# Mixed values made behind the last differential probabilities, output accumulators taken at first use, modulation sums over quadrants in one product per group

## Chip, cores and metric

The kernel runs on one core of one Trainium2 chip. The metric is device microseconds (us) for one execution. The kernel before takes 1186.48 us, the median of three runs (1186.45, 1186.48 and 1188.06). TensorE is called PE below, VectorE DVE, ScalarE ACT, GpSimd POOL, and SyncE SP, whose queue issues most of the loads.

## What is computed

256 tokens of width 1024 go through two blocks, all in float32. The first block has two encoder layers. Each does

```
h    = rmsnorm(x, norm_g[l])
proj = h @ w_in[l]                    # q, k, v, gate of two attentions, 4096 columns
out_a = neighborhood_attention(...)   # 8 heads of 64, a window of 16 columns of a 4 x 64 grid
out_b = diff_attention(...)           # 4 heads: softmax 1 - lam * softmax 2, times v, then rmsnorm
y = concat(out_a * silu(g_a), out_b * silu(g_b))
x = x + y @ w_out[l]
```

The second block has two layers of three sublayers: a SwiGLU feed forward (1024 to 2 x 2816 and back), a mixer (a pooling one in layer 0, attention on shared keys and values in layer 1), and another feed forward. Each sublayer normalizes x and modulates it with a shift, a scale and a gate, which are parts of `silu(c) @ ada_w[layer] + ada_b[layer]`. With the two vectors of the shared keys and values that makes 20 modulation vectors of 1024 values each.

## The kernel before

**Products.** A float32 product is made of three fp32r products: the high part of the activations times the high part of the weights (L1893), low times high (L1898), high times low (L1906). ACT makes the high part of each weight unit (w_hi, L666, a unit is 128 x 2048), and DVE (L1222) or POOL (L535, in four pieces) makes the low part (w_lo = raw - w_hi). `half_step` (L1879) issues one such step of 12 matmuls for one unit and one half of the tokens. A step takes about 2.7 us. Each engine's order is written out by hand; semaphores, named by events, link the engines.

**Encoder layer.** `column_product` (L1938) runs 32 steps s = 0 to 31, four for each of 8 column groups (`IN_GROUPS`, L82): q and k of the differential attention (kind b), v b, q a, k a, v a, gate b, gate a. Group g accumulates in one of two pairs of PSUM banks; `acc_use` (L1857) makes the PE queue wait until the group that used the pair two uses ago is freed. The group v a (g = 5) ends with s = 23. Behind every step each engine does the short work of the attentions that the table `short_work` (L417) puts there, in the same order on all engines. Around the change that is:

- s = 23: `da_pT` of head 3 (the differential probabilities of the last head are transposed by PE, L2073, and copied from PSUM by ACT, L738), then `na_scores` of pair 1.
- s = 24: `da_out` of head 3 (PE, L2106: probabilities times v b; it waits for the copy of s = 23), then `na_pT` of pair 0 (PE L2082, ACT copy L738).
- s = 25: `na_out` of pair 0 (PE, L2094). It waits for event `v_ready` of kind a and for the copy of s = 24. Then `na_scores` of pair 2.

**Mixed values.** The neighborhood attention of a row block reads 128 keys that lie in both token tiles, so beside v a itself (`vv["a"]`, shown as va) two mixed tiles `v_mix` are made from the same PSUM banks. They lie in the memory of the differential queries, so the profile shows them as qbT. ACT makes them in its work at the end of group 5, ahead of everything else of s = 23: two copies of 128 rows (L878), the copy to va (L868 in layer 0, in two halves, L866 in layer 1, in one), then two copies of 32 rows (L878) behind a wait on the first two. Only then comes the copy of the probabilities (L738).

**Output product.** Behind s = 31 the loop behind L2148 takes two pairs of banks, for both token tiles, at its start: the first is freed by `gate_ready` b, the second by `gate_ready` a, which DVE (L1526) signals after ACT's tanh of the last group. It runs eight steps. Between step 0 and step 1, and between 1 and 2, PE transposes the gated neighborhood output (L1990), for which it waits for `y_gated` a (DVE L1416 in layer 0, L1413 in layer 1).

**Modulation sums.** DVE multiplies and adds the rows of `ada_w` by silu(c) (`ada`, L1195), transposes the 128 partial sums of a vector in blocks of 32 x 32 (L1154) and reduces each block (L1157) into `parts`: for partition p and block b a sum over a quarter of the rows. What is left is a sum over the four quadrants of 32 partitions. `FOLDS` (L53) groups the 20 vectors into eight folds of 1 to 4 vectors. For each fold, `fold_sums` (L1915) issues four float32 matmuls with four shifted 128 x 128 views of `fold` (zeros, and a column block that adds up the quadrants) and with every fourth column of `parts`, and DVE's `reduce_vectors` (L1162) adds the bias in one instruction (L1167) and finishes each vector. `fold` is zeroed by POOL and filled by one DVE instruction (`fold_columns`, L1144). The first fold lies behind s = 31 of layer 0, the other seven in the feed forward products.

`job` (L1847) gives the PSUM banks 4, 5 and 6 in turn to the short work; each use waits until the one before on that bank is read.

## Time and profile before

| | us |
|---|---|
| median of three runs | 1186.48 |
| lowest and highest | 1186.45, 1188.06 |
| the profiled execution, device time | 1186.72 |
| its span in the trace | 1184.9 |
| PE busy with matmuls | 1161.9 (98%) |
| DVE busy | 823.6 (70%) |
| ACT busy | 583.4 (49%) |
| POOL busy | 564.6 (48%) |

The profiled execution lies 0.24 us above the median, and 1.8 us of it lie outside the span. A row of a timeline gives the start, the length, the engine, the line, and the instruction with its tiles and their shapes; x4 means that four instructions were merged, and the brackets name the idle time ahead of it and what ended it. PE's rows overlap, since the length of a matmul contains its way through the array: the distance of two starts is the time that it takes up.

### The profile page before, as it was taken

The page shows a single profiled execution, that of the slowest core. Times are in us where ns is not written, and L with a number is a line of the kernel's source. Part 1 is how long each engine was busy: PE and PEld are TensorE (multiplying, and loading weights), DVE is VectorE, ACT ScalarE, POOL GpSimd, SP SyncE. Part 2 cuts the span into 40 slices and gives each one's busy share as a digit, 9 for nine tenths or more (in the row PEclk, how much of TensorE's full clock was granted, in tenths as well). Part 3 has the DMA queues.
Part 4 walks back from the last instruction along what each step waited for, and adds up shares of the span by engine and source line. Part 5 has one row for each costly group of instructions (what it writes and reads, how often), then busy time and mean ns, then how long its engine had stood idle before and what let it go on. Part 6 is the DMA issues. An engine that isn't in the chain of part 4 may idle for free.

```text
span 1184.9 us, 15260 instructions
## 1 busy us (share of the span) xinstructions
PE 1161.9 (98%) x5688; PEld 952.7 (80%) x5688; DVE 823.6 (70%) x1152; ACT 583.4 (49%) x764; POOL 564.6 (48%) x418
## 2 busy tenths in 40 slices
PE   9999999999999999899999999999999999999998
PEld 6777787877788888888887888888888887888887
DVE  6896468856797797778769666797793666645423
ACT  5557564676543443644344267443342766443440
POOL 1365324575364552735535227665351563445360
PEclk9999999999999999999999999999999999999999
DMA  9976379846799997569898658799874534876650
GB/s 349 352 273 223 111 250 333 279 150 221 235 368 323 330 348 292 163 214 344 276 333 313 239 209 285 249 345 301 311 288 143 186 123 160 267 232 203 204 195 36
DMA packets 183833, 297.93 MB, mean 251 GB/s; under 512 B 8464, under 2 KB 102352, under 8 KB 183760
## 3 DMA queue, kind: packets, MB, share of 16 engines
q1 hardware_dynamic: 177696, 284.82, 69.7%
q10 hardware_dynamic: 6064, 12.14, 3.1%
q8 instruction: 46, 0.75, 0.3%
q14 instruction: 27, 0.22, 0.1%
HBM read 294.79 MB, written 2.13 MB: 251 GB/s over the span
## 4 chain that ended last, share of the span: by engine, by line
PE 84%; DVE 8%; ACT 4%; issue 2%; SPq 1%; DMA 1%; POOL 1%; ACTq 0%; DVEq 0%
PE ps L1893 26%; PE ps L1906 25%; PE ps L1898 25%; PE ps L2188 2%; PE ps L1990 1%; DVE w_lo L1222 1%; ACT w_hi L666 1%; DVE ps L1206 1%; DMA raw<-w_in 1%; PE ps L2047 1%; POOL stat L526 1%; PE ps L2106 1%; SPq L492 1%; PE ps L2036 1%; DVE ps L1318 1%
## 5 line engine op out<-in xcount | busy, mean ns | idle before, releaser
L535 POOL TENSOR_TENSOR w_lo<-raw,w_hi 128x512 fp32r<-128x512 f32 x348 | 485.4, 1427 | 428.3 <-ACT w_hi L666 428.1
L666 ACT ACTIVATE w_hi<-raw 128x2048 fp32r<-128x2048 f32 x188 | 354.5, 1909 | 102.3 <-PE ps L1906 68.2
L1893 PE MATMUL ps<-w_hi,h_hi 128*128 128x512 f32 x1120 | 313.0, 401 | 1.0 <-issue 0.8
L1906 PE MATMUL ps<-w_lo,h_hi 128*128 128x512 f32 x1120 | 301.4, 391 | 0.8 <-DVE w_lo L1222 0.4
L1898 PE MATMUL ps<-w_hi,h_lo 128*128 128x512 f32 x1120 | 300.5, 390 | 0.0
L1222 DVE TENSOR_TENSOR w_lo<-raw,w_hi 128x2048 fp32r<-128x2048 f32 x96 | 225.2, 2350 | 103.6 <-ACT w_hi L666 101.3
L1906 PEld LDWEIGHTS ps<-w_lo,h_hi 128*128 128x128 f32 x1120 | 209.3, 188 | 48.4 <-DVE w_lo L1222 2.7
L1898 PEld LDWEIGHTS ps<-w_hi,h_lo 128*128 128x128 f32 x1120 | 210.3, 188 | 45.9 <-DVE h_lo L1282 0.2
L1893 PEld LDWEIGHTS ps<-w_hi,h_hi 128*128 128x128 f32 x1120 | 202.3, 189 | 43.5 <-issue 5.5
L1206 DVE SCALAR_TENSOR_TENSOR ps<-ada_raw,ccol,ps 128x512 f32<-128x512 f32 x240 | 181.1, 754 | 7.9 <-DMA ada_raw<-ada_w 1.1
L950 ACT ACTIVATE a_hi<-ps 128x512 fp32r<-128x512 f32 x44 | 26.4, 599 | 156.4 <-PE ps L2188 156.4
L526 POOL TENSOR_TENSOR stat<-stat,minus_half 128x1 f32<-128x1 f32 (+3 forms) x25 | 29.1, 1166 | 147.9 <-DVE stat L1258 112.3
L1893 PE MATMUL ps<-w_hi,a_hi 128*128 128x512 f32 x348 | 94.0, 392 | 0.0
L1906 PE MATMUL ps<-w_lo,a_hi 128*128 128x512 f32 x348 | 93.1, 389 | 0.0
L1898 PE MATMUL ps<-w_hi,a_lo 128*128 128x512 f32 x348 | 93.1, 389 | 0.0
L1898 PEld LDWEIGHTS ps<-w_hi,a_lo 128*128 128x128 f32 x348 | 65.3, 188 | 13.7
L1906 PEld LDWEIGHTS ps<-w_lo,a_hi 128*128 128x128 f32 x348 | 65.3, 188 | 13.7
L1893 PEld LDWEIGHTS ps<-w_hi,a_hi 128*128 128x128 f32 x348 | 64.6, 188 | 12.9
L960 ACT ACTIVATE hn<-ps 128x512 f32<-128x512 f32 x44 | 26.3, 598 | 92.9 <-PE ps L1906 92.9
L1580 DVE SCALAR_TENSOR_TENSOR hn<-hn,ps 128x512 f32<-128x512 f32 x44 | 30.1, 685 | 45.0 <-ACT hn L960 44.8
L760 ACT ACTIVATE pr<-lg,stat 128x256 f32<-128x256 f32 (+1 forms) x64 | 28.5, 447 | 52.2 <-DVE stat L1366 52.2
L1573 DVE TENSOR_TENSOR a_lo<-ps,a_hi 128x512 fp32r<-128x512 f32 x44 | 30.4, 692 | 32.3 <-ACT a_hi L950 31.2
(209 smaller groups left out, 964.1 us busy)
## 6 DMA issues: line engine op xcount, KB each, us to landing
raw<-ffn_in SPq DMA_DIRECT2D x176, 512.0 KB, 5.9
ada_raw<-ada_w SPq DMA_DIRECT2D x144, 512.0 KB, 7.3
raw<-ffn_out SPq DMA_DIRECT2D x44, 1024.0 KB, 6.6
raw<-w_in SPq DMA_DIRECT2D x31, 1024.0 KB, 8.4
raw<-w_out SPq DMA_DIRECT2D x8, 1024.0 KB, 5.0
ada_raw<-kv_ada_w SPq DMA_DIRECT2D x16, 512.0 KB, 7.9
raw<-w_kv SPq DMA_DIRECT2D x8, 1024.0 KB, 5.7
raw<-w_q SPq DMA_DIRECT2D x4, 1024.0 KB, 5.1
```

The source lines that it names most:

```text
L526: pool.tensor_tensor(st(at, n), st(at, n), minus_half[:, 0:n], ALU.pow).then_inc(*S.inc("rsqrt_ready", *key))
L535: ins = pool.tensor_tensor(w_lo[:, u % RAW, piece], raw[:, u % RAW, piece], w_hi[:, u % RING, piece].bitcast(F32), ALU.subtract)
L666: act.activation(w_hi[:, u % RING, :], raw[:, u % RAW, :], ACT.Copy).then_inc(*S.inc("w_hi_ready", u))
L760: ins = act.activation(pr1[:, w, t, 0:n], lg1[:, s, t, 0:n], ACT.Exp, bias=st(rs + 2 + t), scale=-1.0, accum_out=st(rs + t))
L950: act.activation(a_hi[:, 2 * g:2 * g + 2, :].rearrange("p k c -> p (k c)"), bank(b), ACT.Copy).then_inc(*S.inc("a_hi_ready", name, g))
L1206: ins = dve.scalar_tensor_tensor(out=into, in0=src, scalar=c, in1=acc, op0=ALU.mult, op1=ALU.add)
L1222: dve.tensor_tensor(w_lo[:, u % RAW, :], raw[:, u % RAW, :], w_hi[:, u % RING, :].bitcast(F32), ALU.subtract).then_inc(*S.inc("w_lo_dve", u))
L1573: dve.tensor_tensor(a_lo[sl].rearrange("p k c -> p (k c)"), bank(b), a_hi[sl].rearrange("p k c -> p (k c)").bitcast(F32), ALU.subtract).th ...
L1580: link(dve.scalar_tensor_tensor(out=ffn_gate, in0=ffn_tanh, scalar=1.0, in1=ps[:, b:b + 2, 0:GC], op0=ALU.add, op1=ALU.mult))
L1893: pe.matmul(bank(b), hi[:, k_in_lhs + k, tok], wh[:, k, c * 512:(c + 1) * 512], start=start and k == 0, stop=False)
L1898: pe.matmul(bank(b), lo[:, k_in_lhs + k, tok], wh[:, k, c * 512:(c + 1) * 512], start=False, stop=False)
L1906: ins = pe.matmul(bank(b), hi[:, k_in_lhs + k, tok], wl[:, k, c * 512:(c + 1) * 512], start=False, stop=stop and k == nk - 1)
```

## The change

It does four things. ACT's mixed copies of the values and the event `v_ready` a move from the end of group 5 to behind the copy of the probabilities of the last differential head; va is still copied first. Their order among themselves changes, and there are two waits of ACT on itself in place of one. In the output product, the second pair of banks is asked for at the first step that writes it, which is step 2. `fold` becomes a 128 x 128 matrix that adds up quadrants in all columns at once, made by four DVE instructions in place of POOL's zeroing and one. A fold is one matmul with all columns of `parts`, and its bias is added by four DVE instructions, one for each quadrant of partitions, which pick every fourth column of the sums.

```diff
@@ -270,7 +270,7 @@
         ada_raw = sb("ada_raw", [P, ADA_RING, 2, 512])
         ada_acc = sb("ada_acc", [P, 512])
         parts = sb("parts", [P, 2, 4, D // QUAD])
-        fold = sb("fold", [P, 2 * P])
+        fold = sb("fold", [P, P])
         x = sb("x", [P, NT, D])
         hn = sb("hn", [P, NT, D])
         h_hi = sb("h_hi", [P, KC, T], F32R)
@@ -518,7 +518,6 @@
         @block.gpsimd
         def _(pool):
             pool.memset(minus_half[:], -0.5).then_inc(*S.inc("minus_half_ready"))
-            pool.memset(fold[:], 0.0).then_inc(*S.inc("fold_zeroed"))
             pool.wait_ge(*S.at("minus_half_ready"))
 
             def rsqrt(at, n, *key):
@@ -774,11 +773,28 @@
             act.wait_ge(*S.at("minus_half_ready"))
             act.activation(ccol[:, 1, 0:1], minus_half[:, 0:1], ACT.Exp).then_inc(*S.inc("tables_loaded"))
 
+            def mix_values(layer):
+
+                b = acc_bank["in", layer, IN_GROUPS.index(("v", "a"))]
+
+                def mix(m, t, rows=slice(0, P)):
+                    return act.activation(v_mix[rows, m, :], bank(b + t)[rows], ACT.Copy,
+                                          scale=1.0 if layer else stat[rows, t:t + 1])
+
+                mix(0, 0).then_inc(*S.inc("first_v_mixed", layer))
+                mix(1, 1).then_inc(*S.inc("v_mixed", layer))
+                act.wait_ge(*S.at("first_v_mixed", layer))
+                mix(0, 1, slice(0, 32))
+                act.wait_ge(*S.at("v_mixed", layer))
+                mix(1, 0, slice(96, P)).then_inc(*S.inc("v_ready", layer, "a"))
+
             def encoder_work(layer, s):
                 for what, i in short_work(layer, s):
                     if what == "da_pT":
                         key = ("da", layer, i)
                         copy_pT(pT1[:, i % 2].rearrange("p k q -> p (k q)"), job_bank[("pT", *key)], 512, *key)
+                        if i == HEADS_DA - 1:
+                            mix_values(layer)
                     elif what == "na_pT":
                         key = ("na", layer, i)
                         copy_pT(pT1[:, i % 2].rearrange("p k q -> p (k q)"), job_bank[("pT", *key)], 512, *key)
@@ -874,19 +890,9 @@
                                     act.wait_ge(*S.at("qkT_done", layer, {1: 0, 3: 1, 4: 3}[g], 1))
                                 evacuate(qk_stage).then_inc(*S.inc("qk_staged", layer, g))
                             elif what == "v":
-                                def mix_v(m, t, rows=slice(0, P)):
-                                    return act.activation(v_mix[rows, m, :], bank(b + t)[rows], ACT.Copy,
-                                                          scale=1.0 if layer else stat[rows, t:t + 1])
-
-                                if kind == "a":
-                                    mix_v(0, 0)
-                                    mix_v(1, 1).then_inc(*S.inc("v_mixed", layer))
                                 ins = evacuate(vv[kind][:])
-                                if kind == "a":
-                                    act.wait_ge(*S.at("v_mixed", layer))
-                                    mix_v(0, 1, slice(0, 32))
-                                    ins = mix_v(1, 0, slice(96, P))
-                                ins.then_inc(*S.inc("v_ready", layer, kind))
+                                if kind == "b":
+                                    ins.then_inc(*S.inc("v_ready", layer, kind))
                             else:
                                 evacuate(gg[kind][:], ACT.Tanh, 2, 0.5).then_inc(*S.inc("gate_tanh", layer, kind))
                     encoder_work(layer, s)
@@ -1143,9 +1149,10 @@
 
             def fold_columns():
 
-                dve.wait_ge(*S.at("fold_zeroed"))
-                dve.tensor_reduce(fold[:, P - QUAD:P], ident.rearrange("p (q r) -> p r q", r=QUAD), AX.X,
-                                  ALU.add).then_inc(*S.inc("fold_ready"))
+                every = ident.rearrange("p (q r) -> p r q", r=QUAD)
+                for q in range(P // QUAD):
+                    ins = dve.tensor_reduce(fold[:, q * QUAD:(q + 1) * QUAD], every, AX.X, ALU.add)
+                ins.then_inc(*S.inc("fold_ready"))
 
             def part_sums(v, half):
 
@@ -1164,8 +1171,11 @@
                 these = slice(vecs[0], vecs[-1] + 1)
                 dve.wait_ge(*S.at("folded", n))
                 b = job_bank["fold", n]
-                dve.tensor_tensor(mods[:, these, :], bank(b)[:, 0:len(vecs) * KC].rearrange("p (v k) -> p v k", k=KC),
-                                  bcols[:, these, :], ALU.add).then_inc(*S.inc("biased", n))
+                sums = bank(b)[:, 0:len(vecs) * D // QUAD].rearrange("p (v k q) -> p q v k", k=KC, q=P // QUAD)
+                for q in range(P // QUAD):
+                    rows = slice(q * QUAD, (q + 1) * QUAD)
+                    ins = dve.tensor_tensor(mods[rows, these, :], sums[rows, q], bcols[rows, these, :], ALU.add)
+                ins.then_inc(*S.inc("biased", n))
                 dve.wait_ge(*S.at("biased", n))
                 for v in vecs:
                     m = mods[:, v, :]
@@ -1918,12 +1928,8 @@
                 pe.wait_ge(*S.at("fold_ready"))
                 pe.wait_ge(*S.at("parts_ready", vecs[-1], 1))
                 b = job("fold", (n,), ("biased", n))
-                for j in range(P // QUAD):
-                    at = P - (j + 1) * QUAD
-                    ins = pe.matmul(bank(b)[:, 0:len(vecs) * KC], fold[:, at:at + P],
-                                    parts[:, n % 2, 0:len(vecs), j::P // QUAD], start=j == 0,
-                                    stop=j == P // QUAD - 1)
-                ins.then_inc(*S.inc("folded", n))
+                pe.matmul(bank(b)[:, 0:len(vecs) * D // QUAD], fold[:], parts[:, n % 2, 0:len(vecs), :], start=True,
+                          stop=True).then_inc(*S.inc("folded", n))
 
             def ada_jobs(u):
 
@@ -2145,8 +2151,10 @@
 
                 out_name = ("out", layer)
                 after_name = "a1" if layer == 0 else "fin"
-                b = [acc_use((out_name, t), ("x_ready", after_name, t)) for t in range(NT)]
+                b = {}
                 for s, (i, t) in enumerate(((0, 0), (1, 0), (0, 1), (2, 0), (3, 0), (1, 1), (2, 1), (3, 1))):
+                    if t not in b:
+                        b[t] = acc_use((out_name, t), ("x_ready", after_name, t))
                     half = 1 if i < 2 else 0
                     if s in (1, 2):
                         transpose_half(("y", layer), s - 1, 0, "yT_done", [("y_gated", layer, "a")])
```

## Rows read from the trace of the kernel before

**Rows 1.** Timeline of PE, layer 0, steps 24 and 25.

```profile
97.61 1.53 PE L2106 MATMUL ps<-vb,pT 128*128 128x128 f32 x8 [2.86 <-ACT pT L738]
...
103.47 0.27 PE L2094 MATMUL ps<-va,pT 128*64 128x64 f32 x1
```

**Rows 2.** Timeline of PE, layer 1, the same steps.

```profile
240.07 1.13 PE L2106 MATMUL ps<-vb,pT 128*128 128x128 f32 x8 [2.53 <-ACT pT L738]
...
244.31 0.27 PE L2094 MATMUL ps<-va,pT 128*64 128x64 f32 x1
```

**Rows 3.** Stretches: start:end us, length, busy of five engines, PE clock, DMA share, GB/s.

```profile
97.60:103.50 5.90, 5.89 (x26) 4.91 (x26) 0.28 (x2) 4.91 (x15) 1.62 (x2) 0.71 0.29 103
...
240.00:244.30 4.30, 4.23 (x24) 3.51 (x24) 3.04 (x5) 4.30 (x15) 1.43 (x2) 1.00 0.33 123
...
493.00:498.00 5.00, 4.15 (x23) 4.18 (x23) 2.82 (x6) 2.73 (x5) 4.15 (x4) 0.66 0.01 5
```

**Rows 4.** Timeline of ACT, layer 0, steps 23 and 24.

```profile
93.21 1.24 ACT L878 ACTIVATE qbT<-ps,stat 128x512 f32<-128x512 f32 x2
...
100.14 0.60 ACT L738 ACTIVATE pT<-ps 128x512 f32<-128x512 f32 x1
```

**Rows 5.** Timeline of ACT, layer 1, steps 23 and 24.

```profile
236.28 1.05 ACT L878 ACTIVATE qbT<-ps 128x512 f32<-128x512 f32 x2
237.23 1.01 ACT L866 ACTIVATE va<-ps 128x1024 f32<-128x1024 f32 x1
...
242.32 0.59 ACT L738 ACTIVATE pT<-ps 128x512 f32<-128x512 f32 x1
```

**Rows 6.** Timeline of PE, end of the input product and output product of both layers.

```profile
126.54 0.96 PE L1923 MATMUL ps<-parts,fold 128*128 128x16 f32 x8
128.16 1.16 PE L1893 MATMUL ps<-w_hi,yn_hi 128*128 128x512 f32 x4 [0.66 <-DVE ga L1526]
...
130.99 0.60 PE L1990 MATMUL ps<-ident,hn 128*128 128x128 f32 x4
...
139.56 1.20 PE L1906 MATMUL ps<-w_lo,h_hi 128*128 128x512 f32 x4 [0.19 <-DVE w_lo L1222]
...
268.74 1.15 PE L1893 MATMUL ps<-w_hi,yn_hi 128*128 128x512 f32 x4 [1.21 <-DVE ga L1526]
```

**Rows 7.** Timeline of DVE in the same stretches.

```profile
129.13 1.41 DVE L1416 SCALAR_TENSOR_TENSOR hn<-hn,stat,ga 128x512 f32<-128x512 f32 x2
...
136.81 0.17 DVE L1167 TENSOR_TENSOR mods<-ps,bcols 128x16 f32<-128x16 f32 x1
...
137.21 4.49 DVE L1222 TENSOR_TENSOR w_lo<-raw,w_hi 128x2048 fp32r<-128x2048 f32 x2
...
269.95 1.22 DVE L1413 TENSOR_TENSOR hn<-hn,ga 128x1024 f32<-128x1024 f32 x1
```

**Rows 8.** Timeline of DVE, layer 0: two small instructions without a wait between them.

```profile
88.88 0.15 DVE L1488 RECIPROCAL stat<-stat 128x2 f32<-128x2 f32 x1
88.96 0.26 DVE L1366 CUSTOM_DVE_ANT_0 lg<-ps,bias 128x128 f32<-128x128 f32 x1
```

**Rows 9.** Instructions on tile fold: count, ns least/median/most, first and last start, forms.

```profile
L1923 PE MATMUL ps<-parts,fold x64: 181/263/284, 126.5 to 1097.4; 128*128 128x16 f32 x24, 128*128 128x24 f32 x24, 128*128 128x32 f32 x8, 128*128 128x8 f32 x8
...
L1147 DVE TENSOR_REDUCE fold<-ident x1: 370/370/370, 29.3 to 29.3; 128x32 f32<-128x128 f32 x1
```

**Rows 10.** Timeline of PE: four float32 products of 128 columns, and the second fold.

```profile
226.23 1.05 PE L2106 MATMUL ps<-vb,pT 128*128 128x128 f32 x8
...
360.61 0.98 PE L1923 MATMUL ps<-parts,fold 128*128 128x32 f32 x8
```

**Rows 11.** Timeline of DVE, layer 0, behind fold_columns.

```profile
36.77 1.29 DVE L1447 TENSOR_SCALAR kbT<-ps 128x512 f32<-128x512 f32 x2 [0.94 <-PE ps L2036]
```

**Rows 12.** Timelines of ACT and PE, first down product: w_hi of unit 6, its first use.

```profile
444.00 1.92 ACT L666 ACTIVATE w_hi<-raw 128x2048 fp32r<-128x2048 f32 x1 [6.61 <-DMA raw<-ffn_out]
...
456.97 1.07 PE L1893 MATMUL ps<-w_hi,a_hi 128*128 128x512 f32 x4
```

## The prediction

> **What bounds the kernel.** I read the page first. PE is busy with matmuls for 98% of the span, so a change pays only where PE stops, or where it issues fewer matmuls. Next the waits, and the rows of PE's timeline that have idle time in brackets: there are about twenty, and the two largest are the same place in both encoder layers. The reader should see in [rows 1, 2] that PE stands for 2.86 and 2.53 us in front of the product of the last differential head, and that ACT's copy of the probabilities ends each of these. [Rows 3] hold a second thing: after the stop of layer 0 the granted clock of PE is 0.71 over the stretch, between the levels of 2.4 and 1.2 GHz, and after the like stop of layer 1 it is 1.00. From that product to the first product with mixed values PE takes 103.47 - 97.61 = 5.86 us in layer 0 and 244.31 - 240.07 = 4.24 us in layer 1 [rows 1, 2]. The work is the same, so the lower clock costs 1.62 us. Then I read ACT's timeline for what it did before the copy [rows 4, 5], and the timelines around the output products and the folds.
>
> **Mixed values.** Layer 0: ACT starts the two mixed copies at 93.21 [rows 4], then makes two copies of the same size to va and two of 32 rows, and only then the copy of the probabilities, whose end lets PE go on at 97.61 [rows 1]. After the change only va's stand ahead: 93.21 + 1.14 (the pair's 1.24 less the overlap with the next) + 0.60 = 94.95, and PE goes on at about 95.05 in place of 97.61. PE was free at 97.61 - 2.86 = 94.75, so 0.3 us of the stop is left. At that stop I expect no lower clock, so PE would be at the first mixed product at 95.05 + 4.24 = 99.3. There it is late for the next thing: ACT's copy for pair 0, which ends at 100.14 + 0.60 = 100.74 [rows 4]. Between 93.21 and that copy ACT works without a gap and nothing is taken from it, only reordered; the four mixed copies now lie between the two copies of probabilities and are done before the exponentials, near 97.5, so they are not what PE waits for. PE starts at 100.8 in place of 103.47: **2.7 us**, of which 1.6 is clock and 1.05 is the stop. A new stop of 1.5 us is what is left. Layer 1: ACT is free at 236.28, va takes 1.01 and the copy 0.60 [rows 5], so PE starts at about 237.95, passes through its 4.24 us to 242.2, and waits for the copy that ends at 242.32 + 0.59 = 242.91: 242.97 in place of 244.31, **1.3 us**. The second wait of ACT on itself is covered by the copy between; if it isn't, it costs some 0.1 to 0.4 us in each layer, because ACT's chain to the second copy has no slack.
>
> **Accumulators at first use.** Layer 0: PE stops for 0.66 us in front of step 0 of the output product [rows 6]. Step 0 and its neighbours take 130.99 - 128.16 = 2.83 us. It could now start at about 126.9 and end at 129.7, but the transposes behind it need the gated output, which DVE finishes at 129.13 + 1.41 = 130.54 [rows 7], a chain that the change leaves as it is. They start at 130.6 in place of 130.99: 0.35 us. Layer 1: start 268.74 - 1.21 = 267.53, end 270.4, DVE ready at 269.95 + 1.22 = 271.17 [rows 6, 7]; before it was 268.74 + 2.83 = 271.57, so **0.3 us**. In layer 0 the 0.35 is spent at 139.56, where PE waits for a low part that DVE starts at 137.21, right behind the bias of the first fold at 136.81 [rows 6, 7]. DVE's chain moves forward by 0.35 with the transposes and back by three more bias instructions. The trace has none on a quadrant of partitions. One takes 0.17 us here; the nearest pair without a wait starts 0.08 apart [rows 8]. So three cost between 0.25 and 0.5 us, and I take 0.35, near the middle: the low part comes as before, and layer 0 gains **0**, the first fold's saving included, as it lies in the same stop.
>
> By [rows 8] alone, with 0.08 us each, layer 0 would gain 0.1 us. The Trainium skill, "VectorE: DVE Perf Modes", section "Two Vector instructions with no wait between them", says against this edit that an instruction whose operands start in another quadrant of partitions than those before is held until all earlier ones have finished. By that rule each of the three takes its whole 0.17 us, 0.5 in all, and layer 0 loses 0.15 us. No row of this trace has such a pair.
>
> **Folds.** There are eight, each with eight records of L1923, between 126.5 and 1097.4 [rows 9]: four float32 matmuls, two records each. The second [rows 10] is 0.98 long; less the last record's own 0.27, that is seven distances of 0.101, so a fold takes up 0.81 us of PE. One matmul is two records: 0.20 us. The moving columns grow from 8 to 32 up to 32 to 128, and the product of 128 columns in [rows 10] says what that costs: 1.05 against 0.98 for four matmuls, 0.02 each. So a fold takes 0.20 to 0.22 and saves 0.6. If the last matmul showed a way through the array that the others hid, it would save 0.4 at the least; if the distances shrank, 0.66 at the most. The seven folds behind the first lie in feed forward products without a stop: 7 x 0.6 = **4.2 us**, bounds 2.8 to 4.6.
>
> **Costs taken as nothing.** fold_columns: three more of 0.37 us [rows 9] on DVE, 1.1 us at 29.3; before 36.77 DVE waits 0.94 us for PE [rows 11] and a little more for a load ahead of that; without this cover PE would see up to 0.2. Seven times three bias instructions in the feed forward products, 0.35 us each time, lie in DVE's idle time (70% busy, and no stop of PE ends there); POOL's zeroing at the start is far from any reader. No DMA is added or moved except the two bias loads that ACT issues at step 23: they come up to 1 us later behind the self-waits, and their readers are at step 25, 5 us on.
>
> **Sum.** 2.7 + 1.3 + 0 + 0.3 + 4.2 = 8.5 us. The profiled execution took 1186.72, so 1178.2; it lies 0.24 above the median, so **1178.0 us**.
>
> **Rivals.**
> *The clock stays low in layer 0.* The stop of 0.3 and the new one of 1.5 us lie within 6 us. For it: a stop of 2.86 lowered the clock. Against: one of 2.53 did not. Price 1.6: 1179.6. Chance 0.12.
> *The other low stretch goes too.* At 493 to 498 the clock is 0.66 [rows 3], about 5 x 0.34 = 1.7 us lost, in the pooling mixer. The change doesn't touch it, but it comes 6 us earlier, and of three stops above 2.2 us two lowered the clock. 1176.3. Chance 0.18.
> *The savings of the folds are given back to the loads.* In the first down product ACT waits 6.61 us for a weight unit [rows 12], so memory paces that stretch. Against: its high part is ready at 445.9, and PE needs it at 456.97, 11 us of slack. If it were so, the 4.2 would be gone, 1182.2. Chance 0.08. With it, at 0.04, that ACT's self-waits and smaller folds cost 2 us together: 1180.
> *Slower.* The change leaves more and shorter stops: 0.3 and 1.5 in layer 0, 0.4 and 0.8 in layer 1, and about 0.9, 0.5 and 0.9 in the two output products. If each lowered the clock as the one at 97.6 did, seven times 1.6 = 11.3 us would be lost: 1189.3. That decides from the point at which stops below 1.5 us lower the clock. Against: step 0 behind the stops of 0.66 in [rows 6] runs at its usual pace. Chance 0.03.
>
> **How the numbers follow.** The forecast has 0.55. With the two clock cases it has 0.85, and their prices with half a microsecond on either side give 1175.6 to 1181.2. About 0.2% (2.4 us) can be told from no change: only the slower rival and a few mishaps together end within or above it. Faster 0.95, same 0.03, slower 0.02.
>
> **What would show it.** The stop before L2106 falls to 0.3 us, and a stop of 1.5 (0.8) us in front of L2094, released by L738, appears. The clock of the stretch is 1.00. The transposes behind step 0 start 0.3 us nearer to the end of the input product, released by DVE. The folds have two records and take up 0.2. A PE stop behind POOL or DVE w_lo in steps 25 to 29, or less than 3 us gained over the seven folds, would make the prediction wrong.

## The result and the profile after

| | before | after |
|---|---|---|
| median, us | 1187.61 (6 runs, 1186.45 to 1188.62) | 1178.01 (6 runs, 1177.49 to 1178.54) |
| ratio of the times | | 0.9922, 95% interval 0.9911 to 0.9932 |
| profiled execution, device time and span | 1186.72, 1184.9 | 1177.49, 1175.7 |

The changed kernel takes the 1178.0 us of the forecast and is 0.8% faster than the kernel before. The gain is larger than forecast, 9.6 us by these medians against 8.5, because three more runs of the kernel before moved its median from 1186.48 to 1187.61. Why it varies so much is a result of the experiments.

The page of the changed kernel has 48 fewer records of PE, in matmuls and in weight loads, and 27 more of DVE:

```profile
PE 1155.3 (98%) x5640; PEld 945.4 (80%) x5640; DVE 835.9 (71%) x1179; ACT 583.2 (50%) x764; POOL 562.9 (48%) x417
```

These are PE's rows of the changed kernel in layer 0 that answer to [rows 1, 6]; L2112 is the product of the last differential head, L2100 the first mixed product, L1996 the transposes, L1903, L1908 and L1916 the three kinds of a weight product:

```profile
94.58 1.13 PE L2112 MATMUL ps<-vb,pT 128*128 128x128 f32 x8 [0.34 <-ACT pT L737]
...
100.24 0.24 PE L2100 MATMUL ps<-va,pT 128*64 128x64 f32 x1 [1.08 <-ACT pT L737]
...
123.28 0.33 PE L1931 MATMUL ps<-parts,fold 128*128 128x64 f32 x2
123.43 1.17 PE L1903 MATMUL ps<-w_hi,yn_hi 128*128 128x512 f32 x4
...
127.33 0.66 PE L1996 MATMUL ps<-ident,hn 128*128 128x128 f32 x4 [0.91 <-DVE hn L1426]
...
136.49 1.20 PE L1916 MATMUL ps<-w_lo,h_hi 128*128 128x512 f32 x4 [0.72 <-DVE w_lo L1232]
```

And in layer 1, which answer to [rows 2, 6]:

```profile
234.81 1.13 PE L2112 MATMUL ps<-vb,pT 128*128 128x128 f32 x8 [0.34 <-ACT pT L737]
...
238.43 1.19 PE L1916 MATMUL ps<-w_lo,h_hi 128*128 128x512 f32 x4 [0.20 <-POOL w_lo L534]
240.11 0.24 PE L2100 MATMUL ps<-va,pT 128*64 128x64 f32 x1 [0.49 <-ACT pT L737]
...
267.01 0.66 PE L1996 MATMUL ps<-ident,hn 128*128 128x128 f32 x4 [0.93 <-DVE hn L1423]
```

The stops of 2.86 and 2.53 us have become 0.34 each, and behind each stands a new one in front of the first mixed product, 1.08 and 0.49 us. In the output products PE now waits behind step 0, for DVE's gated output (hn), and no longer ahead of it, for the gate (ga): 0.93 in place of 1.21 us in layer 1, but 0.91 in place of 0.66 in layer 0. The stop before the low part has grown from 0.19 to 0.72 us. PE comes to these places earlier than before, so a longer stop there is not a loss by itself. ACT's timeline in layer 0 has the new order, va, the copy of the probabilities, three and one mixed copies, the copy of pair 0:

```profile
92.72 1.24 ACT L884 ACTIVATE va<-ps,stat 128x512 f32<-128x512 f32 x2
93.86 0.58 ACT L737 ACTIVATE pT<-ps 128x512 f32<-128x512 f32 x1
94.33 1.80 ACT L781 ACTIVATE qbT<-ps,stat 128x512 f32<-128x512 f32 x3
...
96.14 0.68 ACT L781 ACTIVATE qbT<-ps,stat 32x512 f32<-32x512 f32 x1
...
99.49 0.60 ACT L737 ACTIVATE pT<-ps 128x512 f32<-128x512 f32 x1
```

The stretches that answer to [rows 3], columns as there (PE's clock is the figure behind the busy times of the five engines): 1.00 in both encoder layers, and still low in the pooling mixer, 0.63.

```profile
94.58:100.24 5.66, 4.58 (x25) 3.43 (x25) 2.42 (x11) 5.60 (x19) 3.33 (x3) 1.00 0.76 286
234.80:240.10 5.30, 4.61 (x24) 3.43 (x25) 4.14 (x7) 5.24 (x19) 3.58 (x3) 1.00 0.57 215
489.40:494.00 4.60, 4.56 (x25) 4.56 (x26) 2.56 (x4) 2.91 (x6) 4.60 (x4) 0.63 0.00 0
```

The folds: all instructions on the tile in the first fence (columns as in [rows 9]), the second fold and the fifth in PE's timeline in the second, and DVE's bias of the first fold in the third.

```profile
L1931 PE MATMUL ps<-parts,fold x16: 190/272/275, 123.3 to 1088.2; 128*128 128x64 f32 x6, 128*128 128x96 f32 x6, 128*128 128x128 f32 x2, 128*128 128x32 f32 x2
L1154 DVE TENSOR_REDUCE fold<-ident x4: 379/383/394, 28.8 to 29.6; 128x32 f32<-128x128 f32 x4
```

```profile
356.13 0.38 PE L1931 MATMUL ps<-parts,fold 128*128 128x128 f32 x2
356.35 0.60 PE L2196 MATMUL ps<-ident,hn 128*128 128x128 f32 x4
...
655.72 0.35 PE L1931 MATMUL ps<-parts,fold 128*128 128x96 f32 x2
655.86 1.18 PE L1903 MATMUL ps<-w_hi,a_hi 128*128 128x512 f32 x4
```

```profile
133.20 0.71 DVE L1177 TENSOR_TENSOR mods<-ps,bcols 32x16 f32<-32x16 f32 x4
133.94 0.17 DVE L1188 SCALAR_TENSOR_TENSOR mods<-mods,gcols 128x8 f32<-128x8 f32 x1
134.14 4.49 DVE L1232 TENSOR_TENSOR w_lo<-raw,w_hi 128x2048 fp32r<-128x2048 f32 x2
```

Subtracting the starts of the same work in the two traces shows where the time went:

| point | before | after | earlier by | new since the last point |
|---|---|---|---|---|
| PE free behind step 24, layer 0 | 94.75 | 94.24 | 0.51 | 0.51 |
| first mixed product, layer 0 | 103.47 | 100.24 | 3.23 | 2.72 |
| low part of output unit 2, layer 0 | 139.56 | 136.49 | 3.07 | -0.16 |
| PE free behind step 24, layer 1 | 237.54 | 234.47 | 3.07 | 0 |
| first mixed product, layer 1 | 244.31 | 240.11 | 4.20 | 1.13 |
| transposes of the output product, layer 1 | 271.55 | 267.01 | 4.54 | 0.34 |
| end of the span | 1184.9 | 1175.7 | 9.2 | 4.7, for seven folds |

The first 0.51 us is taken as no part of the change: the first six records of PE take 4.64 us in this execution and 5.09 in the other, and in the executions profiled below 4.38 to 5.49. (The first two of them take 2.07 us; two of the same shape at 6.83 us take 1.02.) The other 8.7 us are the change.

### The profile page after: what moved, and what is told of

The parts are those of the page before. It is cut to its first block, busy times and chain, and to the rows that moved or that the text cites. A ratio compares the mean times of both kernels' runs of the same rounds, so it can differ in the third digit from the quotient of the medians.

```text
span 1175.7 us, 15187 instructions
## 1 busy us (share of the span) xinstructions
PE 1155.3 (98%) x5640; PEld 945.4 (80%) x5640; DVE 835.9 (71%) x1179; ACT 583.2 (50%) x764; POOL 562.9 (48%) x417
## 4 chain that ended last, share of the span: by engine, by line
PE 83%; DVE 8%; ACT 4%; issue 2%; SPq 1%; DMA 1%; POOL 1%; ACTq 0%; DVEq 0%
PE ps L1903 25%; PE ps L1916 25%; PE ps L1908 25%; PE ps L2196 2%; PE ps L1996 2%; DVE w_lo L1232 1%; ACT w_hi L665 1%; DVE ps L1216 1%; DMA raw<-w_in 1%; PE ps L2053 1%; POOL stat L525 1%; SPq L492 1%; PE ps L2042 1%; DVE ps L1328 1%; DVE x L1329 1%
## 5 line engine op out<-in xcount | busy, mean ns | idle before, releaser
L1903 PE MATMUL ps<-w_hi,h_hi 128*128 128x512 f32 x1120 | 312.1, 400 | 1.1 <-issue 0.8
L1916 PE MATMUL ps<-w_lo,h_hi 128*128 128x512 f32 x1120 | 301.6, 391 | 1.6 <-DVE w_lo L1232 1.0
L1908 PE MATMUL ps<-w_hi,h_lo 128*128 128x512 f32 x1120 | 300.3, 390 | 0.0
L1916 PEld LDWEIGHTS ps<-w_lo,h_hi 128*128 128x128 f32 x1120 | 209.1, 188 | 50.0 <-DVE w_lo L1232 3.3
L1908 PEld LDWEIGHTS ps<-w_hi,h_lo 128*128 128x128 f32 x1120 | 210.2, 188 | 45.7 <-DVE h_lo L1292 0.2
L1903 PEld LDWEIGHTS ps<-w_hi,h_hi 128*128 128x128 f32 x1120 | 201.8, 188 | 43.5 <-issue 5.5
L1903 PE MATMUL ps<-w_hi,a_hi 128*128 128x512 f32 x348 | 94.1, 392 | 0.0
L1908 PE MATMUL ps<-w_hi,a_lo 128*128 128x512 f32 x348 | 93.1, 389 | 0.0
L1916 PE MATMUL ps<-w_lo,a_hi 128*128 128x512 f32 x348 | 93.1, 389 | 0.0
L1908 PEld LDWEIGHTS ps<-w_hi,a_lo 128*128 128x128 f32 x348 | 65.3, 188 | 13.7
L1916 PEld LDWEIGHTS ps<-w_lo,a_hi 128*128 128x128 f32 x348 | 65.3, 188 | 13.7
L1903 PEld LDWEIGHTS ps<-w_hi,a_hi 128*128 128x128 f32 x348 | 64.6, 188 | 12.9
```

What stands on the lines that cost most here:

```text
L1903: pe.matmul(bank(b), hi[:, k_in_lhs + k, tok], wh[:, k, c * 512:(c + 1) * 512], start=start and k == 0, stop=False)
L1908: pe.matmul(bank(b), lo[:, k_in_lhs + k, tok], wh[:, k, c * 512:(c + 1) * 512], start=False, stop=False)
L1916: ins = pe.matmul(bank(b), hi[:, k_in_lhs + k, tok], wl[:, k, c * 512:(c + 1) * 512], start=False, stop=stop and k == nk - 1)
```

## The experiments

All times are medians, and each kernel ran beside the kernel before on the same chip. Beside mix_undone, stop_filled, acc_undone and folds_undone that one took 1187.88 us (15 runs, 1185.65 to 1188.93), beside bias_by_columns and the three reordered kernels 1186.41 (7 runs), beside mix_undone_filled and dve_mixer_filled 1186.73 (9 runs). The changed kernel was not run again beside them. Differences from its 1178.0 us are between groups of runs, and where they are under 1 us the traces decide.

### One part undone at a time

**mix_undone**: the mixed values made ahead of the copy of the probabilities again.

```diff
...
-                        if i == HEADS_DA - 1:
-                            mix_values(layer)
...
+                                if kind == "a":
+                                    mix_v(0, 0)
+                                    mix_v(1, 1).then_inc(*S.inc("v_mixed", layer))
                                 ins = evacuate(vv[kind][:])
-                                if kind == "b":
-                                    ins.then_inc(*S.inc("v_ready", layer, kind))
+                                if kind == "a":
+                                    act.wait_ge(*S.at("v_mixed", layer))
+                                    mix_v(0, 1, slice(0, 32))
+                                    ins = mix_v(1, 0, slice(96, P))
+                                ins.then_inc(*S.inc("v_ready", layer, kind))
```

> The changed kernel with the mixed values made ahead of the copy of the last differential probabilities again. Theory (each part pays where its stop was): PE stops for 2.5 to 2.9 us before the product of the last differential head in both layers, the stop of 1.1 us before the first mixed product is gone, and the time is 1178.0 + 2.7 + 1.1 = 1181.8 us if the clock falls behind the stop of layer 0 (0.71 over the next 5.9 us), 1180.2 if it falls behind neither. Rival (the order alone matters and the clock would have fallen anyway): the stretch behind the stop has the clock of the changed kernel, 1.00, and 1180.2 in every execution.

Measured: 1182.21 us (1180.65 to 1182.41), ratio to the kernel before 0.9951 (0.9939 to 0.9964). That is 4.2 us over the changed kernel. The timeline of PE and the stretches behind the two stops:

```profile
97.17 2.05 PE L2105 MATMUL ps<-vb,pT 128*128 128x128 f32 x8 [2.86 <-ACT pT L737]
...
239.70 1.63 PE L2105 MATMUL ps<-vb,pT 128*128 128x128 f32 x8 [2.53 <-ACT pT L737]
```

```profile
97.00:103.00 6.00, 5.83 (x28) 5.07 (x30) 0.18 (x1) 5.05 (x16) 1.20 (x2) 0.73 0.31 112
...
239.00:244.00 5.00, 4.30 (x18) 3.94 (x19) 3.78 (x6) 4.72 (x16) 2.06 (x2) 0.66 0.43 161
```

In this execution the clock falls behind both stops, in layer 1 too, where the profile of the kernel before had 1.00 [rows 3]. From 97.20 to 99.50 it is 0.50, the level of 1.2 GHz. The profile of bias_by_columns (below), which has the same stops as the kernel before, shows both falls as well: from the product behind the stop to the first mixed product it takes 5.90 and 5.84 us, where 4.24 is the time at the full clock. So in the three profiles with these stops unfilled the clock fell three times of three in layer 0 and twice of three in layer 1: whether it falls is decided anew in each execution. Two falls are more loss than the theory had, which had one; the 1180.65 of the quickest run fits the 1180.2 without one.

**stop_filled** puts the clock to the test in the kernel before, by keeping PE busy in the stop. Its two products in each layer go to a bank that is not used yet; they are not part of the computation.

```diff
                         key = ("da", layer, h)
+                        if h == HEADS_DA - 1:
+                            for _ in range(2):
+                                pe.matmul(bank(acc_bank["in", layer, 6] + 1), ident[:], x[:, 0, 0:512], start=True, stop=True)
                         pe.wait_ge(*S.at("v_ready", layer, "b"))
```

> The kernel before, with two float32 products of 512 columns (about 0.85 us each) between step 24 and the product of the last differential head, into a bank that is not in use yet. Nothing that PE waits for changes. Theory (the stop itself lowers the clock): PE is busy for 1.7 of the 2.9 us, the clock stays 1.00 behind it, and PE goes from that product to the first mixed one in 4.2 us in layer 0 in place of 5.9: 1.6 us less than the kernel before wherever that one had the lower clock. Rival (the clock falls for another reason, such as the loads that fill this stretch): the clock behind the stop is still 0.71, and the time is that of the kernel before.

Measured: 1184.94 us (11 runs, 1184.55 to 1185.61), ratio 0.9981 (0.9972 to 0.9989): 2.9 us less by the medians and 2.4 by the means, for four products more. PE's timeline, and the stretch behind the stop:

```profile
94.86 1.88 PE L2103 MATMUL ps<-x,ident 128*128 128x512 f32 x4
97.88 1.13 PE L2109 MATMUL ps<-vb,pT 128*128 128x128 f32 x8 [1.14 <-ACT pT L738]
```

```profile
97.60:103.50 5.90, 5.62 (x57) 4.64 (x58) 1.12 (x4) 5.02 (x16) 1.81 (x2) 1.00 0.33 120
```

The product starts as late as before, 97.88 with a beginning 0.27 us later, and takes 1.13 in place of 1.53. The load traffic in the stop is the same, 403 GB/s here (94.70 to 98.00) and 405 in the kernel before (94.70 to 97.60), so the rival falls: what lowers the clock is that PE stands still. In layer 1 the clock was 1.00 here too, as in the one profile of the kernel before. The runs also explain the kernel before. Filled, it varies by 1.1 us; unfilled by 3.3 us. Its 15 runs lie in two groups, five at 1185.65 to 1186.44 and ten at 1187.21 to 1188.93, whose medians lie 1.5 us apart, about the price of one fall. The execution with one fall in the encoder layers took 1186.72 us, the one of bias_by_columns with two 1188.40. That most executions of the kernel before have two is inferred from this, as only one of them was profiled.

**mix_undone_filled**: both edits in one kernel, the old order without the low clock.

> The kernel mix_undone (1182.2 us) with the two float32 products of stop_filled in the stop before the product of the last differential head, in both layers. It has the old order without the lower clock, so it parts the 4.2 us of the mixed values into order and clock. Theory from the traces (order 1.1 us in each layer, the rest clock): 1178.0 + 2.2 = 1180.2 us, clock 1.00 behind both stops. Rival (nearly all is clock, as the 2.9 us of stop_filled say): 1179.3 us or less.

Measured: 1180.00 us (1179.68 to 1180.51), ratio 0.9938 (0.9925 to 0.9950). The stretches behind the stops:

```profile
97.20:103.00 5.80, 5.40 (x56) 4.48 (x56) 0.63 (x4) 5.15 (x16) 1.70 (x2) 1.00 0.34 126
239.00:244.00 5.00, 5.00 (x55) 4.08 (x54) 2.93 (x6) 4.28 (x13) 1.64 (x2) 1.00 0.12 39
```

So of the 4.2 us that moving the mixed values is worth, 1180.0 - 1178.0 = 2.0 are order and 1182.2 - 1180.0 = 2.2 are clock. The traces agree in the main: from the end of step 24 in layer 0 to PE's stop of 0.84 us behind the output product of layer 1 (at 289.03 in the changed kernel) it is 200.2 us in mix_undone with two falls, 197.3 here and 194.8 in the changed kernel, so 2.5 order and 2.9 clock. The rival, nearly all clock, falls.

**acc_undone**: both pairs of banks asked for ahead of the output product again.

```diff
-                b = {}
+                b = [acc_use((out_name, t), ("x_ready", after_name, t)) for t in range(NT)]
...
-                    if t not in b:
-                        b[t] = acc_use((out_name, t), ("x_ready", after_name, t))
```

> The changed kernel with both pairs of banks asked for ahead of the output product again. Theory: PE stops in front of step 0 for DVE's gate in place of stopping behind it for the gated output; the transposes start 0.3 us later in each layer, 1178.6 us. Rival (the stop has only moved): no difference, 1178.0, the transposes in both at DVE's time.

Measured: 1178.22 us (1177.39 to 1178.66), ratio 0.9919 (0.9905 to 0.9932), which can't be told from the changed kernel. The timeline can:

```profile
94.81 1.13 PE L2112 MATMUL ps<-vb,pT 128*128 128x128 f32 x8 [0.33 <-ACT pT L737]
...
125.16 1.17 PE L1903 MATMUL ps<-w_hi,yn_hi 128*128 128x512 f32 x4 [1.28 <-DVE ga L1536]
137.09 1.20 PE L1916 MATMUL ps<-w_lo,h_hi 128*128 128x512 f32 x4 [0.73 <-DVE w_lo L1232]
```

From the last differential head to the low part it is 137.09 - 94.81 = 42.28 us here and 136.49 - 94.58 = 41.91 in the changed kernel: 0.37. The same subtraction in layer 1, from 235.43 to 289.94 here and from 234.81 to 289.03 there, gives 0.29. Together that is the 0.6 of the theory, seen in the traces of one execution each; the medians differ by 0.2 and their ranges overlap, so the times show neither it nor the rival. In layer 0 the earlier transposes bring DVE's chain forward by this 0.37 us, where the prediction had 0.35, and the three bias instructions use it up again.

**folds_undone**: four matmuls and one bias instruction again.

```diff
...
-                for q in range(P // QUAD):
-                    rows = slice(q * QUAD, (q + 1) * QUAD)
-                    ins = dve.tensor_tensor(mods[rows, these, :], sums[rows, q], bcols[rows, these, :], ALU.add)
-                ins.then_inc(*S.inc("biased", n))
+                dve.tensor_tensor(mods[:, these, :], bank(b)[:, 0:len(vecs) * KC].rearrange("p (v k) -> p v k", k=KC),
+                                  bcols[:, these, :], ALU.add).then_inc(*S.inc("biased", n))
...
-                pe.matmul(bank(b)[:, 0:len(vecs) * D // QUAD], fold[:], parts[:, n % 2, 0:len(vecs), :], start=True,
-                          stop=True).then_inc(*S.inc("folded", n))
+                for j in range(P // QUAD):
+                    at = P - (j + 1) * QUAD
+                    ins = pe.matmul(bank(b)[:, 0:len(vecs) * KC], fold[:, at:at + P],
+                                    parts[:, n % 2, 0:len(vecs), j::P // QUAD], start=j == 0,
+                                    stop=j == P // QUAD - 1)
+                ins.then_inc(*S.inc("folded", n))
```

> The changed kernel with four matmuls per fold and one bias instruction again. Theory: the seven folds of the feed forward products cost 0.6 to 0.67 us each again, 4.2 to 4.7 us; in layer 0 the stop before the low part (0.72 us) shrinks by the 0.5 us of three bias instructions, so 1181.9 to 1182.4 us. Rival (the feed forward products are paced by their loads, or the folds are hidden): less than 2 us, 1180 or less.

Measured: 1181.63 us (1181.05 to 1182.06), ratio 0.9948 (0.9936 to 0.9961), 3.6 us over the changed kernel, 0.3 under the lower end of the theory. PE's timeline has the second fold and the low part, DVE's the bias:

```profile
136.19 1.20 PE L1913 MATMUL ps<-w_lo,h_hi 128*128 128x512 f32 x4 [0.17 <-DVE w_lo L1229]
...
355.82 0.98 PE L1930 MATMUL ps<-parts,fold 128*128 128x32 f32 x8
356.63 0.64 PE L2197 MATMUL ps<-ident,hn 128*128 128x128 f32 x4
```

```profile
133.45 0.16 DVE L1174 TENSOR_TENSOR mods<-ps,bcols 128x16 f32<-128x16 f32 x1
```

The stop before the low part is 0.17 in place of 0.72 us: the three bias instructions cost 0.55 where DVE is waited for. With the seven folds that leaves (3.6 + 0.55) / 7 = 0.6 us each by the medians. The traces give 0.67: in a stretch that holds three folds this kernel takes 320.90 us (628.94 to 949.84) and the changed one 318.89 (627.99 to 946.88). This kernel's profile had the full clock in the mixer, which the changed kernel's had not and which is worth 0.7 us (below). That could be the difference between 0.6 and 0.67, but the clock of the other executions is not known.

### The price of a bias on quadrants

**bias_by_columns** is the kernel before, with four instructions that each take a quarter of the columns on all partitions.

```diff
-                dve.tensor_tensor(mods[:, these, :], bank(b)[:, 0:len(vecs) * KC].rearrange("p (v k) -> p v k", k=KC),
-                                  bcols[:, these, :], ALU.add).then_inc(*S.inc("biased", n))
+                sums = bank(b)[:, 0:len(vecs) * KC].rearrange("p (v k) -> p v k", k=KC)
+                for q in range(4):
+                    ks = slice(q * KC // 4, (q + 1) * KC // 4)
+                    ins = dve.tensor_tensor(mods[:, these, ks], sums[:, :, ks], bcols[:, these, ks], ALU.add)
+                ins.then_inc(*S.inc("biased", n))
```

> The kernel before with the bias of each fold added in four instructions as in the changed one, but on all 128 partitions and a quarter of the columns each, so that all start in the same quadrant of partitions. In the changed kernel the four instructions on quadrants start about 0.18 us apart. Theory (each was held until the one before had finished, because it starts in another quadrant): here they start 0.07 to 0.10 us apart. Rival (four small instructions on a PSUM source are that slow anyway): 0.17 to 0.20 us apart here too.

It took 1188.40 us in the only execution, so nothing follows from its time. DVE's timeline:

```profile
136.59 0.36 DVE L1170 TENSOR_TENSOR mods<-ps,bcols 128x4 f32<-128x4 f32 x4
136.97 0.17 DVE L1181 SCALAR_TENSOR_TENSOR mods<-mods,gcols 128x8 f32<-128x8 f32 x1
```

Four take 0.38 us up to the next instruction. One takes 0.20 in the kernel before, from 136.81 [rows 7] to this row:

```profile
137.01 0.17 DVE L1178 SCALAR_TENSOR_TENSOR mods<-mods,gcols 128x8 f32<-128x8 f32 x1
```

So three more cost 0.18, 0.06 each. On quadrants four take 0.74 and three more cost 0.54, 0.18 each. These two sets differ in size as well, 4 columns here and 16 there. Other folds of the same traces have equal sizes. Four instructions of 8 columns take 0.73 us on quadrants (last fold of the changed kernel, first fence) and 0.41 on all partitions (second fold of bias_by_columns, second fence):

```profile
1090.44 0.69 DVE L1177 TENSOR_TENSOR mods<-ps,bcols 32x8 f32<-32x8 f32 x4
1091.17 0.17 DVE L1192 TENSOR_SCALAR mods<-mods 128x8 f32<-128x8 f32 x1
```

```profile
368.51 0.38 DVE L1170 TENSOR_TENSOR mods<-ps,bcols 128x8 f32<-128x8 f32 x4
368.92 0.17 DVE L1185 TENSOR_SCALAR mods<-mods 128x8 f32<-128x8 f32 x1
```

So the size does not make it. One difference is left beside the quadrant: on quadrants the source columns lie four apart in PSUM, here side by side, and no run parts the two. The Trainium skill, "VectorE: DVE Perf Modes", section "Two Vector instructions with no wait between them", has it that an instruction that starts in another quadrant than the ones before waits until all earlier ones have finished. The 0.18 us from start to start agree with that, as one such instruction takes 0.17 us by itself.

### Attacking the stops that are left

**act_reordered**: at step 24 ACT copies the probabilities of pair 0 ahead of its work on the last differential output.

```diff
-                for what, i in short_work(layer, s):
+                work = short_work(layer, s)
+                if s == DA_OUT[-1]:
+                    work.sort(key=lambda w: w[0] == "da_out")
+                for what, i in work:
```

> The changed kernel, with ACT's copy of pair 0's probabilities at step 24 made ahead of its four instructions on the last differential output in place of behind them. Theory (ACT's chain is what PE waits for in front of the first mixed product): the copy ends 0.95 us earlier, the stop there falls from 1.08 to 0.1 us in layer 0 and from 0.49 to 0 in layer 1, 1176.6 us. Rival (the banks bind): the scores of pair 2 wait for the bank of the differential output instead, and 0.3 us or more of it comes back in each layer, 1177.2 or above.

Measured: 1177.20 us (4 runs, 1176.89 to 1177.88), ratio 0.9920 (0.9905 to 0.9934): 0.8 us less than the changed kernel, at the rival's end, with ranges that overlap (1177.49 to 1178.54 there). PE's timeline:

```profile
100.31 0.33 PE L2071 MATMUL ps<-kaT,qaT 64*64 64x128 f32 x2 [0.24 <-issue]
113.83 1.19 PE L1919 MATMUL ps<-w_lo,h_hi 128*128 128x512 f32 x4 [0.23 <-POOL w_lo L534]
115.80 0.66 PE L1999 MATMUL ps<-ident,hn 128*128 128x128 f32 x4 [0.16 <-DVE hn L1445]
...
289.10 1.17 PE L1906 MATMUL ps<-w_hi,h_hi 128*128 128x512 f32 x4 [0.84 <-issue]
```

The stop of 1.08 us before the mixed product is gone, and 0.24 + 0.23 + 0.16 = 0.63 of it comes back in three places: in front of the scores of pair 2 (by the code they wait for the bank of the differential output; the profile names no releaser), and at POOL's and DVE's chains, which did not move. The rest of it is lost by the output product, where the stop of 0.91 us behind DVE (at 127.48 here) is the same in both kernels. From the product of the last differential head in layer 0 to PE's stop of 0.84 us behind the output product of layer 1 it is 289.10 - 94.69 = 194.41 us here and 289.03 - 94.58 = 194.45 in the changed kernel. The spans of the two traces differ by 0.6 us because of the clock in the mixer, 1.00 here: from that stop to the transposes at 627.99 us in the changed kernel (627.39 here) it is 338.29 us here and 338.96 there. So between the two profiled executions the gain is clock, and the reordering by itself gave nothing. Whether the medians differ for the same reason is not shown.

**dve_reordered**: DVE's order at step 31 and behind it.

```diff
...
+                    if s == GATE_AT["a"]:
+                        encoder_work(layer, s, True)          # na_out of the last pair, ahead of the gate
...
-                    if s != GATE_AT["b"]:
+                    if s not in (GATE_AT["a"], GATE_AT["b"]):
...
                 gate_na(layer)
+                encoder_work(layer, GATE_AT["a"], False)      # the low part of the second tile
...
+                lows(o + 2)
                 for n in sum_step.get((layer, 31), []):
                     reduce_vectors(n)
```

> The changed kernel, with DVE's order at step 31 changed: the division of the last neighborhood pair ahead of the gate, the low part of the second tile behind the gated output, and the low part of output unit 2 ahead of the bias of the first fold. Theory (DVE's order sets both stops in the output products): the stops in front of the transposes (0.91 and 0.93 us) and in front of the low part in layer 0 (0.72) go, 2.5 us, so 1175.5 us. Rival (ACT's tanh and DVE's gate are already the floor): the stops fall by 0.4 us each at most, 1176.8 or above.

Measured: 1174.81 us (4 runs, 1174.74 to 1175.27), ratio 0.9899 (0.9885 to 0.9914), 3.2 us under the changed kernel. The transposes behind step 0 have no stop in either layer, and in layer 0 one of 0.16 us is left, at another low part:

```profile
126.78 0.66 PE L2002 MATMUL ps<-ident,hn 128*128 128x128 f32 x4
...
138.15 1.19 PE L1922 MATMUL ps<-w_lo,h_hi 128*128 128x512 f32 x4 [0.16 <-DVE w_lo L1232]
```

The theory had 2.5 us. Between the same two points as above it is 287.08 - 94.94 = 192.14 us, 2.3 less than in the changed kernel, and from there to the transposes at 625.36 it is 338.28, 0.7 less. The second part is the mixer: its stretch was at the full clock in this kernel's profile and at the low one in the changed kernel's. So the reordering is worth 2.3 us in the traces, near the theory.

**all_reordered**: both.

> Both reorderings together. Theory: the gains add, 3.9 us, 1174.1 us. Rival (they meet at the same POOL or ACT chain later in the encoder layer): less than 3 us, above 1175.

Measured: 1174.91 us (4 runs, 1174.34 to 1175.42), ratio 0.9898 (0.9881 to 0.9914). The gains do not add: the 0.8 of act_reordered is not seen on top. The stops before the scores of pair 2, behind POOL and behind DVE have the same sizes as in act_reordered (0.24, 0.24, 0.16 in layer 0), so what was left there was small. In the traces the two encoder layers take 286.77 - 94.88 = 191.89 us, 0.25 less than in dve_reordered: with DVE's stops gone, ACT's reordering does give something. But this kernel's profile has the low clock in the mixer, and up to the transposes at 625.96 it takes 339.19 us, 0.9 more than dve_reordered. The clock hides a gain of a quarter of a microsecond. By the medians the two kernels can't be told apart.

**dve_mixer_filled**: dve_reordered with two products, no part of the computation, in the stop of the pooling mixer.

```diff
             mix_across()
+            for _ in range(2):
+                pe.matmul(bank(job_bank["mix", 0, 1]), ident[:], bands.rearrange("p g i c -> p (g i c)")[:, 0:512],
+                          start=True, stop=True)
             mix(1)
```

> The kernel dve_reordered (1174.8 us) with two such products in the stop of 2.27 us of the pooling mixer (at about 486 us), into a bank that nobody uses then. Theory (that stop lowers the clock in some executions and costs 0.6 to 1 us there): the clock behind it is 1.00 in the profile, and the median is 0.3 to 0.8 us less, 1174.3 us, with the highest run below 1174.9. Rival (the two products delay the mixer, or nothing is lost there): 1174.8 us or more.

Measured: 1174.87 us (4 runs, 1174.63 to 1174.95), ratio 0.9894 (0.9879 to 0.9909): the rival's number. PE's row behind that stop, of this kernel and then of dve_reordered:

```profile
486.16 1.13 PE L2015 MATMUL ps<-bands,hn 128*128 128x128 f32 x8 [0.55 <-DVE hn L1657]
```

```profile
486.11 1.13 PE L2015 MATMUL ps<-bands,hn 128*128 128x128 f32 x8 [2.27 <-DVE hn L1657]
```

The stop is 0.55 in place of 2.27 us and nothing is delayed, but nothing is gained either. dve_reordered had the full clock there in its profile, and perhaps in most of its runs. The theory stays unproven for this stop. That the clock falls behind it in some executions is shown: of the eleven profiles in which it is unfilled, seven have the low clock there (the kernel before, the changed kernel, acc_undone, stop_filled, mix_undone_filled, bias_by_columns and all_reordered, 0.63 to 0.75 over the 4.65 us from the second product on), and four the full one.

## Why the prediction was right, point by point

**Mixed values, layer 0: forecast 2.7, measured 2.72.** The stop is 0.34 us (0.3 forecast), and the new one in front of the mixed product 1.08 (1.5 forecast). The forecast counted from start to start, which gives 100.24 - 94.58 - 4.24 = 1.42 us. The figure in the brackets leaves out the last product's way to its end, 0.2, and 0.14 of the time stands ahead of the low part at 97.96. The clock is 1.00, as forecast, and 1.62 us of the gain is from it. That share was taken from the one execution that was profiled.

**Layer 1: forecast 1.3, measured 1.13.** ACT's chain has become a little longer: from PE's free time to the end of the second copy it was 242.91 - 237.54 = 5.37 us before, and is 239.96 - 234.47 = 5.49 now, 0.12 more, the low end of the range that the forecast set aside for ACT's self-waits. In layer 0 ACT's chain from its first copy to its last is 7.37 us in place of 7.53, so that the self-waits are the cause is not shown. The stop of 0.20 behind POOL was named as a thing that would make the prediction wrong. It is there, so that sign was badly chosen: the stop costs nothing, as PE waits for ACT right behind it.

**What the forecast missed here** is that layer 1 loses clock too, in two of the three profiles with its stop unfilled. "After the like stop of layer 1 it is 1.00" was read as a fact of the place; mix_undone shows 0.66 behind the same stop, and the median of the kernel before rose from 1186.48 to 1187.88 as more runs were made. The term that was too small is this clock term: 1.6 us in the sum, 2.2 by mix_undone and mix_undone_filled, and by stop_filled 2.9 (medians) or 2.4 (means). The time of the changed kernel came out right all the same, because the forecast took the gain off the one profiled execution and counted that execution's single fall.

**Accumulators: forecast 0.3, in the traces 0.34 in layer 1.** In layer 0 the forecast was 0, with a loss of 0.15 if the Trainium skill's rule on quadrants held. The loss is 0.16, as by that rule: 0.37 gained by the accumulators (acc_undone) less 0.54 for the bias. "I take 0.35, near the middle" was the wrong choice between the bounds of 0.25 and 0.5: it is 0.54, over the upper end.

**Folds: forecast 4.2, bounds 2.8 to 4.6, measured 4.7 between the traces and 4.1 by the medians** (3.6, with the 0.55 us of the bias added back). The four matmuls take 0.81 us, as worked out from the rows, and the one of 128 columns 0.22 (356.13 to 356.35), which saves 0.59. The narrower ones were priced too high: 0.14 at 96 columns (655.72 to 655.86) in place of 0.20, which saves 0.67. Six of the seven folds are that narrow or narrower, and 0.59 + 6 x 0.67 = 4.6 is what the traces give, at the upper bound.

**Costs taken as nothing** were nothing: DVE's four instructions for the fold matrix take 1.27 us, the idle time before the copy of the keys falls from 0.94 [rows 11] to 0.41 us, and no stop of PE follows up to the one of 0.70 us at 59, which the kernel before has too.

**The rivals.** The low clock did not stay in layer 0. In the mixer it did not go away; its price was set too high at 1.7 us, since DVE ends PE's waits there: between the traces of the changed kernel (low) and of folds_undone (full), over 478 to 629 us and with one fold taken out, it is 0.7, and between all_reordered and dve_reordered 0.9 from PE's stop at 289 us on. The loads did not take back the folds. No stop of 1.3 us or less was followed by a low clock, so the slower case did not begin.

**The sum and the range.** The traces give 2.72 + 1.13 - 0.16 + 0.34 + 4.7 = 8.7 us where the forecast had 8.5: the folds gave 0.5 more than forecast, the mixed values of layer 1 and the output product of layer 0 about 0.2 less each. That the median meets the forecast to 0.01 us is luck. The clock in the mixer, low in the one profile of this kernel and worth 0.7 to 1.0 us, is decided anew in each execution as well. The bounds 1175.6 and 1181.2 do not come out of the sentence on them: the prices of the two clock cases with half a microsecond on either side give 1175.8 and 1180.1. The result lies in both.

## What to carry to other kernels

When one engine is 98% busy, list its few stops with their releasers, and for each write down who is the next to be late: that is what a reordering leaves, and here its size was forecast to about 0.4 us each time. Count the clock into the price of a stop of TensorE such as those of 2.3 to 2.9 us here, and take it from several executions, not one; two useless products in the stop show what share it has. Before a difference of 1 us between two kernels is put down to an edit, compare the traces stage by stage: between the traces of act_reordered and the changed kernel the gain stands at a place that the edit does not touch. A small VectorE instruction on the path cost three times as much here (0.18 us against 0.06) when it started in another quadrant of partitions than the one before.

## What the runs showed of the hardware that was not expected

- A stop of 2.27 to 2.86 us lowers TensorE's granted clock from the level of 2.4 GHz to that of 1.2 GHz in some executions and not in others: behind the 2.86 us in layer 0 in three profiles of three, behind the 2.53 us in layer 1 in two of three, behind the 2.27 us in the mixer in seven of eleven. With 1.7 us of it filled, it stayed at 1.00 in all four places in the encoder layers, and in the one in the mixer. A fall costs 1.5 to 1.7 us in the encoder layers, where PE is what everything waits for, and 0.7 to 1.0 in the mixer.
- Most of the spread of the kernel before comes from this: 3.3 us (1185.65 to 1188.93), against 1.1 us when the two stops are filled.
- Four more float32 products of 512 columns, two in each stop, made a kernel 2.9 us faster by the medians and 2.4 by the means.
- Of a float32 matmul with its own weights, 32, 64 and 96 columns take the same 0.14 us of PE, and 128 columns 0.22.
